# A Griffin-style encoder layer on one core: two first blocks swapped, the end of the up stage reordered, and eight of eighteen sets of DRAM sums made during it

## The reference

```
xn     = rms_norm(x, norm_mix_g)
proj   = xn @ w_in                       # q, k, v of mixer A and of mixer B
att_a  = windowed GQA: 16 query heads, 4 key heads, ALiBi, sinks
att_b  = chunked attention: 16 heads, relative-position bias
gates  = sigmoid(xn @ w_gate)
merged = gates[:, :2048] * (att_a @ w_branch_a) + gates[:, 2048:] * (att_b @ w_branch_b)
h      = x + merged @ w_out
u      = square(relu(rms_norm(h, norm_mlp_g) @ w_mlp_in))      # 2048 -> 8192, "up"
h      = h + u @ w_mlp_out                                     # 8192 -> 2048, "down"
out    = rms_norm(h, norm_final_g)
```

## Time and profile before

| | |
|---|---|
| time, median of 3 runs | 2495.39 us (2495.18 to 2496.13) |
| the profiled execution | 2495.8 us, its span 2493.9 us |
| TensorE busy | 2469.7 us |
| VectorE, ScalarE, GpSimd busy | 1648.4, 1062.1, 193.6 us |
| DMA, mean over the span | 204 GB/s |

### The profile page before, as it was taken

How to read it: one execution, slowest core, us unless ns; L and a number is a source line. 1 busy time by engine, 2 the same in 40 slices (tenths; PEclk the granted TensorE clock), 3 DMA queues, 4 the chain that set the end, 5 groups by cost and what they waited for, 6 DMA issues and landing times.

```text
span 2493.9 us, 34706 instructions
## 1 busy us (share of the span) xinstructions
PE 2469.7 (99%) x14226; PEld 2185.0 (88%) x14226; DVE 1648.4 (66%) x2242; ACT 1062.1 (43%) x1380; POOL 193.6 (8%) x185
## 2 busy tenths in 40 slices
PE   9999999999999999999999999999999999999997
PEld 8898888998888888888899999999998888888886
DVE  5566555556333333523788888888869888877897
ACT  5566765556222222312444333333335444444445
POOL 0011100000011000001000000000011011110010
PEclk9999999999999999999999999999999999999999
DMA  7788898898898999952444344443468666566652
GB/s 260 198 242 250 241 243 248 232 253 227 226 257 250 244 252 251 266 174 97 145 135 128 127 136 136 129 134 128 135 225 326 234 228 223 191 227 231 233 190 106
DMA packets 202082, 508.71 MB, mean 204 GB/s; under 512 B 13616, under 2 KB 126400, under 8 KB 190928
## 3 DMA queue, kind: packets, MB, share of 16 engines
q1 hardware_dynamic: 189120, 355.65, 42.6%
q0 software_dynamic: 12672, 151.00, 23.9%
q10 hardware_dynamic: 144, 0.02, 0.0%
HBM read 485.61 MB, written 172.01 MB: 264 GB/s over the span
## 4 chain that ended last, share of the span: by engine, by line
PE 94%; DVE 2%; DMA 2%; ACT 1%; issue 1%; POOL 0%; SPq 0%; DVEq 0%; ACTq 0%; POOLq 0%
PE bank L1604 30%; PE bank L1606 30%; PE bank L1605 30%; PE bank L1682 1%; PE bank L1717 1%; PE bank L1696 1%; DMA landing<-in_w_out 1%; POOL raw_forms L1510 0%; DMA landing<-in_w_in 0%; DVE up_lo L1327 0%; DVE form_lo_b L1295 0%; DMA raw_forms<-hidden_rows 0%; ACT q_twice L697 0%; ACT w_hi L643 0%; DVE at_lo L1182 0%
## 5 line engine op out<-in xcount | busy, mean ns | idle before, releaser
L974 DVE TENSOR_TENSOR w_lo<-landing,w_hi 128x1024 fp32r<-128x1024 f32 x200 | 248.8, 1244 | 468.1 <-ACT w_hi L643 468.0
L643 ACT ACTIVATE w_hi<-landing 128x1024 fp32r<-128x1024 f32 x200 | 212.0, 1060 | 587.7 <-PE bank L1606 575.7
L857 ACT ACTIVATE up_hi<-up_raw 128x1792 fp32r<-128x1792 f32 x128 | 218.1, 1704 | 407.2 <-PE bank L1606 404.5
L904 ACT ACTIVATE ring<-down_raw 128x1024 fp32r<-128x1024 f32 x224 | 237.5, 1061 | 310.4 <-PE bank L1606 310.4
L1604 PE MATMUL bank<-xn_hi,w_hi 128*128 128x512 f32 x928 | 365.1, 393 | 2.3 <-DVE w_lo L974 1.7
L1606 PE MATMUL bank<-xn_hi,w_lo 128*128 128x512 f32 x928 | 361.9, 390 | 0.0
L1605 PE MATMUL bank<-xn_lo,w_hi 128*128 128x512 f32 x928 | 361.7, 390 | 0.0
L1407 DVE TENSOR_TENSOR ring<-down_raw,ring 128x1024 fp32r<-128x1024 f32 x224 | 285.3, 1283 | 68.2 <-ACT ring L904 68.2
L1327 DVE TENSOR_TENSOR up_lo<-up_raw,up_hi 128x1792 fp32r<-128x1792 f32 x128 | 260.4, 2034 | 88.7 <-ACT up_hi L857 88.7
L1604 PE MATMUL bank<-ring,down_forms 128*128 128x512 f32 x656 | 255.4, 389 | 3.3 <-DVE mix L1349 1.9
L1606 PE MATMUL bank<-ring,down_forms 128*128 128x512 f32 x656 | 255.2, 389 | 0.0
(11 more groups left out here) (183 smaller groups left out, 4809.7 us busy)
## 6 DMA issues: line engine op xcount, KB each, us to landing
down_totals<-in_down_blocks POOLq DMA_DIRECT2D x64, 1024.0 KB, 9.7
up_raw<-in_up_units SPq DMA_DIRECT2D x128, 512.0 KB, 3.4
down_raw<-down_totals SPq DMA_DIRECT2D x128, 512.0 KB, 4.5
down_raw<-in_down_blocks SPq DMA_DIRECT2D x96, 512.0 KB, 4.3
landing<-in_w_in SPq DMA_DIRECT2D x72, 512.0 KB, 6.2
landing<-in_w_gate SPq DMA_DIRECT2D x64, 512.0 KB, 6.0
landing<-in_w_out SPq DMA_DIRECT2D x32, 512.0 KB, 3.7
hidden_rows<-hidden_out SPq DMA_DIRECT2D x32, 512.0 KB, 3.4
```

Of the source, the lines that this page charges most:

```text
L643: nc.scalar.activation(w_hi[:, u % SPLIT, :], landing[:, u % LAND, :], ACT.Copy).then_inc(unit_hi, 1)
L857: nc.scalar.activation(up_hi[n % 2], up_raw[n % 3][:, 1:8, :], ACT.Copy).then_inc(up_hi_done, 1)
L904: nc.scalar.activation(ring[i % RING][:, 0, :], raw_of(i), ACT.Copy).then_inc(piece_hi, 1)
L974: nc.vector.tensor_tensor(w_lo[:, s, :], landing[:, u % LAND, :], w_hi[:, s, :].bitcast(F32), ALU.subtract).then_inc(unit_lo, 1)
```

## The change

1. In `BLOCKS` the second and third block change places: q of A (heads 0 to 3) comes before v of A.
2. At the end of up, for the last unit (127), `first_product` of sub 30 goes ahead of `up_high` on ScalarE, and the first of the four form sums and `mixed_products` of sub 30 go ahead of `up_low` on VectorE.
3. Three of the four form sums of the first down step (forms 1, 2, 4) are made by VectorE (`first_block_sum`), the fourth still by GpSimd, which now waits until three pieces are used. On VectorE and ScalarE the first pieces, forms and the rest of the last two subs' work stand in another order. Later steps keep their sums on GpSimd.
4. Ten sets of DRAM sums (two for up, eight for down steps) run in the mixer stage, one each 16 units; the other eight begin when up unit 8, 20, 32 and so on up to 92 have been used, one each 12 units. GpSimd's `form_sums` for the up stage stands between the two groups.

```diff
--- before.py
+++ after.py
@@ -54,7 +54,7 @@
 
 
 
-BLOCKS = ([("k", "a", 0), ("v", "a", 0), ("q", "a", 0), ("q", "a", 1), ("k", "b", 0), ("q", "a", 2),
+BLOCKS = ([("k", "a", 0), ("q", "a", 0), ("v", "a", 0), ("q", "a", 1), ("k", "b", 0), ("q", "a", 2),
            ("v", "b", 0), ("q", "a", 3), ("g", "a", 0), ("g", "b", 0), ("q", "b", 0)]
           + [(kind, "b", g) for g in (1, 2, 3) for kind in "qkv"]
           + [("g", "a", 1), ("g", "b", 1)])
@@ -874,13 +874,15 @@
                                      accum_out=squares[:, t, q:q + 1]).then_inc(squared, 1)
 
             for n in range(UP_UNITS):
+                if n == UP_UNITS - 1:
+                    first_product(SUBS - 2)
                 up_high(n)
                 if n in (3, 4):
                     for kp in (2 * n - 2, 2 * n - 1):
                         form_high(kp)
                 if n >= 8 and n < 8 + SQUARED_H:
                     sum_squares(n - 8)
-                if n >= 2 and UP_ORDER[n - 2][1] == 3:
+                if n >= 2 and UP_ORDER[n - 2][1] == 3 and n < UP_UNITS - 1:
                     first_product(UP_ORDER[n - 2][0])
 
             def form_split_hi(c, f):
@@ -912,12 +914,16 @@
 
             for i in range(PIECES * STEPS):
                 m, p = i // PIECES, i % PIECES
-                if m == 0 and p % 2 == 0:
+                if i == 0:
+                    form_split_hi(0, 0)
+                    form_split_hi(0, 1)
+                elif m == 0 and p >= 6 and p % 2 == 0:
                     form_split_hi(0, p // 2)
+                piece_high(i)
                 if i == 1:
-                    act.wait_ge(up_used, UP_UNITS)
                     first_product(SUBS - 1)
-                piece_high(i)
+                elif i == 3:
+                    form_split_hi(0, 2)
                 if m % 2 == 1 and m < STEPS - 1:
                     for f in FORMS_AT.get(p, ()):
                         form_split_hi(m // 2 + 1, f)
@@ -1374,7 +1380,25 @@
             up_low(1)
             for k in range(12, 16):
                 form_block(k)
+            def first_block_sum(f):
+
+                k = places[0]
+                if f == 1:
+                    dve.wait_ge(blocks_landed[2], 16)
+                    dve.wait_ge(blocks_landed[3], 16)
+                    a, b = token_block[:], raw_form[k[6]]
+                elif f == 2:
+                    dve.wait_ge(blocks_landed[0], 16)
+                    dve.wait_ge(block_summed, 1)
+                    a, b = raw_form[k[1]], raw_form[k[0]]
+                else:
+                    a, b = raw_form[k[0]], token_block[:]
+                nc.vector.tensor_tensor(raw_form[k[f]], a, b, ALU.subtract).then_inc(block_summed, 1)
+
             for n in range(2, UP_UNITS):
+                if n == UP_UNITS - 1:
+                    first_block_sum(1)
+                    mixed_products(SUBS - 2)
                 up_low(n)
                 if n == 2:
                     form_sums(0, 2, 5)
@@ -1382,7 +1406,7 @@
                 if n in (3, 4):
                     for kp in (2 * n - 2, 2 * n - 1):
                         form_low(kp)
-                if UP_ORDER[n - 2][1] == 3:
+                if UP_ORDER[n - 2][1] == 3 and n < UP_UNITS - 1:
                     mixed_products(UP_ORDER[n - 2][0])
                 if n > 2 and UP_ORDER[n - 3][1] == 3:
                     fourth_block(UP_ORDER[n - 3][0])
@@ -1454,16 +1478,23 @@
 
             for i in range(PIECES * STEPS):
                 m, p = i // PIECES, i % PIECES
-                if m == 0 and p % 2 == 0:
-                    if p == 2:
-                        mixed_products(SUBS - 1)
-                        fourth_block(SUBS - 1)
+                if i == 0:
+                    fourth_block(SUBS - 2)
+                    first_block_sum(2)
+                    first_block_sum(4)
+                    form_split_lo(0, 0)
+                elif i == 1:
+                    hidden(SUBS - 2)
+                    form_split_lo(0, 1)
+                elif m == 0 and p >= 6 and p % 2 == 0:
                     form_split_lo(0, p // 2)
                 piece_low(i)
-                if i == 0:
-                    fourth_block(SUBS - 2)
-                    hidden(SUBS - 2)
-                if i == 5:
+                if i == 1:
+                    mixed_products(SUBS - 1)
+                    fourth_block(SUBS - 1)
+                elif i == 3:
+                    form_split_lo(0, 2)
+                elif i == 6:
                     hidden(SUBS - 1)
                 if i % 2 == 0 and i >= 4:
                     g = i // 2 - 2
@@ -1559,11 +1590,15 @@
                     pool.wait_ge(totals_copied, 16 * (4 * m + 4))
                     added(blocks[3], sums[3])
 
-            for m in range(2 + STEPS):
-                pool.wait_ge(unit_used, 12 + 8 * m if m < 10 else 84 + 10 * (m - 9))
+            for m in range(10):
+                pool.wait_ge(unit_used, 12 + 16 * m)
                 for part in range(6):
                     totals(m, part)
             form_sums()
+            for m in range(10, 2 + STEPS):
+                pool.wait_ge(up_used, UP_END + 12 * (m - 10))
+                for part in range(6):
+                    totals(m, part)
 
             def block_sum(c, f):
 
@@ -1590,8 +1625,9 @@
                     pool.wait_ge(piece_used, PIECES * m + 2 * products)
                     block_sum(m // 2 + 1, f)
 
-            for f in (1, 2, 4, 5):
-                block_sum(0, f)
+            pool.wait_ge(block_summed, 3)
+            pool.wait_ge(piece_used, 3)
+            block_sum(0, 5)
             for m in range(STEPS):
                 for products, f in enumerate((1, 2, 4, 5)):
                     next_sum(m, f, products + 1)
```

## The result

The changed kernel takes 2562.78 us (median of 4, 2560.5 to 2564.4) against 2495.76 us of the kernel before (4 runs): 1.0269 times, with an interval of 1.0257 to 1.0281. It is 67 us slower, where +35 was predicted (2530 us, range 2502 to 2553). The direction and the place were right; the size was not.

A forecast was written before the change was run, and what follows sets the result against it. TensorE, busy 2469.7 of 2493.9 us, was taken as the bound. First blocks -4.3, end of up -0.3, fewer mixer sets -0.5 and eight sets +40 sum to +34.9 us on 2495.39: 2530 us, range 2502 to 2553.

The forecast's parts named there:

- What bounds the kernel, and the mechanism: TensorE bounds; in up, accumulating pairs delay a store and the load behind it, so VectorE's up_lo comes late.
- Eight sets: Beside up: each set costs 4.2 us idle plus 0.8 for the clock, +40 us in all, bounds +16 to +60.
- Landing of the load: Up stage: the load behind the store lands near t 25.7, needed by t 21.5, so 4.2 us idle per set.
- The single accumulating transfers later in a set: Up stage: half the pair, with 7 us for a load to land, so counted as nothing.
- The clock: Up stage: a fall costs about 1.7 us; half was taken, 0.8 us per set.
- The upper bound of 7.5 a set: Up stage: longest pair, load caught again by the third copy (2.9 us), full clock fall: about 7.5 us per set.
- Rival 3: Up stage: two loads of each set late and the clock falls each time, 8 us a set, 2554 us; chance 0.09.
- Rivals 1 and 2: Up stage: rival 1; and second, a quicker pair, stalls of 1 to 2 us per set, 2502 us, chance 0.14.
- rival 1: Up stage: loads still land in time, only wins stay, 2490 us, or 2494 with half a us per set; chance 0.11.
- First blocks: Q before v removes TensorE's wait for q_twice and the low clock behind it: -4.3 us, bounds -2.5 and -4.3.
- Fewer sets in the mixers: Mixer stage: ten sets at half the pace instead of eighteen shorten waits for w_lo: -0.5 us, bounds 0 and -0.6.
- End of up: Passage from up into down: 3.8 us idle go, 0.4 + 0.9 + 2.2 come: -0.3 us, bounds -2.5 and +1.5.

The follow-up runs named there:

- e5: The changed kernel with each of the eight sets beside up started two up units later: 2563.84 us, 1.027.
- e3: The kernel before with only the second and third block swapped (q before v): 2492.46 us, 0.9984.
- e4: The kernel before with only the new end of up and the form sums of the first down step: 2496.79 us, 1.0001.
- e1: The kernel before with only the sets moved (ten in the mixers at half the pace, eight beside up): 2563.02 us, 1.0272.
- e7: The changed kernel with the stores of hidden of the middle subs sent on ScalarE's queue: 2557.38 us, 1.0249.
- e10: The changed kernel with plain copies in place of the accumulating transfers of the eight sets beside up: 2516.57 us, 1.0074.
- e9: e7 with 4096 instead of 8192 bytes in the packets of all accumulating transfers: 2537.69 us, 1.017.
- e11: The changed kernel with VectorE's sums of unit n + 1, instead of n + 2, behind up_lo of unit n: 2539.32 us, 1.0174.
- e2: The changed kernel with all eighteen sets in the mixers, as before: 2493.06 us, 0.9989.
- e6: The changed kernel with the second accumulating transfer of a pair waiting for the first in the eight sets beside up: 2547.76 us, 1.0211.
- e13: e11 with all eighteen sets in the mixers: 2529.37 us, 1.013.
- e14: The changed kernel with the edits of e7 and e6 together, accumulating packets of 8192 bytes: 2544.87 us, 1.0193.

## Why the prediction was wrong in size

- **What bounds the kernel, and the mechanism: right.** Eight gaps ended by `up_lo`, 67 to 71 us apart, VectorE waiting before its sums for `up_raw`, the load behind the store taking 13.4 us, a clock below 1. The prediction's chain holds to a tenth: load lands at t 27.6, plus 3.7 of sums and `up_lo`, is t 31.3, where TensorE goes on (1568.50 - 1537.23).
- **"Eight sets": the term that failed, in size.** It gave 8 x (4.2 + 0.8) = 40 us; it measured 67 to 70, 8.4 to 8.7 a set. In parts:
  - Landing of the load: t 25.7 predicted, from a pair that ends at t 24.3 and a load 1.5 behind it as in the mixers. Here the pair ended at t 25.0 and the load 2.6 later. The 1.5 us came from a load behind a load; behind a store of 1 KB packets there is more left to move when the pair is over (328 of its 512 packets). Main gap 5.5 us in the mean instead of 4.2. The set of 1537 is one of the larger ones (6.4).
  - "The single accumulating transfers later in a set ... I count them as nothing": the gaps beside the main ones make up 50.6 - 43.9 = 6.7 us, 0.8 a set. Of these 2.9 come from the first set's two copies, for which the prediction had no term; the single accumulating transfers have the rest, half a us a set. e5 shows what they cost in another place.
  - The clock: 0.8 a set predicted, half of one fall of 3.4 us. It fell in every set, and in six of eight was at 0.50 for 6.8 us, part of which TensorE stood idle anyway. 13.1 us, 1.6 a set.
  - Idle time and clock are 6.3 + 1.6 = 7.9 a set, and the part of each gap that idle time doesn't count (see "By stage") about 0.5.
  - The upper bound of 7.5 a set was added up too low. By its own terms the longest pair (26.4 less 0.4 for the reaction), the load 1.5 behind it, need by t 21.5, and a full fall of 1.7 give 26.0 + 1.5 - 21.5 + 1.7 = 7.7, and with the 2.9 of the third copy 10.6 a set, +85 us in all. With all of its terms the bound holds the measured 8.5; as it was added up, it doesn't.
- **Rival 3** (two late loads, 8 us a set, 2554 us) came nearest in time but by another way: the load near t 9.4 (issued at 1546.39) took only 3.2 us: it had landed at 1549.60, as the pair's packets began. The three causes above did it together. Rivals 1 and 2 fell: the loads were not in time, and the stalls were not of 1 to 2 us. The rule of the Trainium skill on turns of some 9 to 17 descriptors ("DMA: Bandwidth & Descriptors", Queues, rings and completion order) would have given rival 1. The trace disagrees with it again: 116 to 117 packets, a load of 13.4 us, and in e5 loads' packets in waves 0.8 us apart, which is the time of one packet of each queue (last section).
- **First blocks: right.** -4.3 predicted, -3.5 measured (e3, interval -1.7 to -6.2), the wait itself gone as worked out. The 0.8 between them is less than a wait for `w_lo` varies from one execution to another (0.40 to 2.47 us), with or without the swap.
- **Fewer sets in the mixers: not contradicted.** The part ahead of up is 5.3 us shorter in the profiled executions, where -4.3 - 0.5 was predicted. Half a us can't be told from it, but the mechanism is there: the wait for `w_lo` near 1070 us is gone, which was 0.40 us in the trace that the term was read from and 2.47 in e4's. e1, with ten sets and no swap, has the border at 1218.1 us, 1.0 earlier than before; e4 has it at 1222.6, after its 2.47 us and 3.41 us of low clock behind them. So the term was read from one execution that had the wait short.
- **End of up: right in its waits.** Predicted idle times 0.4, 0.9 and 2.2; measured 0.35, 0.57 and 2.35, and e4 as a whole is 1.0001. Not in the prediction: behind the 2.35 the clock was low for 3.4 us (1946.80 to 1950.21), which costs some 1.6 and makes most of the +1.9 behind up. It isn't a fixed price (last section).

## What to carry to other kernels

Before moving background transfers beside a stage, read not the mean share of the DMA engines but what the dearest packet does to the load in the next queue: here accumulating packets of 0.64 us turned loads of 3.4 us into 9 to 14, at a DMA share of only 0.42. Then ask what stands behind that load in a fixed queue: in another order of VectorE's queue the same sets cost 1.2 instead of 8.7 us each, but that order put two engines in series and cost 36 us by itself. And when one stall's price is carried over to longer stalls, the clock's part must be taken as a range that includes a longer fall than the one seen, and an upper bound must be added up from all of the terms that it names.

## What the runs showed of the hardware

- A plain load and an accumulating transfer on another queue took turns packet for packet wherever they were counted, with packets of 1 KB (a store), 2 KB and 4 KB (loads) beside accumulating ones of 8 KB. In e5, 1424.5 to 1428.5 us, with the loads' 4 KB packets:

```profile
q0 software_dynamic: 80, 0.66, 78.5%
q1 hardware_dynamic: 82, 0.34, 22.2%
```

  These are 16 x 4 x 0.785 / 80 = 0.63 us for an accumulating packet and 0.17 for one of a load, together 0.80; the loads' packets come in waves of about 16, 0.8 us apart, one to each DMA engine.
- So a lone load in the middle of a pair lands when the pair ends (10.8 us in e5) instead of after 3.4. With the store on a third queue (e7) the three take one packet each in turn, 104, 110 and 108, and the load takes 11.3.
- The clock around a stall. In the changed kernel it was at 0.50 for 6.83 us with six of the eight main gaps, beginning within the gap, and for 3.41 with those of 4.15, 4.44 and 2.35 us. The length of a gap alone doesn't tell. In e10 the clock was low after gaps of 1.77 and 2.40 us and stayed at 1.00 through one of 2.50 and one of 2.85, and in the changed kernel through one of 2.92. The wait of 2.35 us before piece 4 is the same in eleven traces: the clock fell behind it in six (the changed kernel, e4, e7, e9, e10, e11) and stayed at 1.00 in five (e2, e5, e6, e13, e14).
